# A trunk layer in three-pass float32 matmuls: rows for the MLP and gate stages turned by VectorE's 32x32 blocks and sixteen on-chip transfers instead of by TensorE

## Chip, cores and metric

One core of a Trainium2 chip. The metric is the device time of one execution in microseconds (us), the median of several runs.

## What is computed

One layer of a trunk for 256 tokens of width D = 2048, all in float32. The mixer is an attention with a compressed, a selected and a window branch; the change leaves it alone. After it come an MLP of width 8192 with a squared ReLU, and a gate on a projection of a 256-wide side input:

```python
def rms_norm(x, g):
    y = x * lax.rsqrt(jnp.mean(x * x, axis=-1, keepdims=True) + EPS)
    return y * g

h = x + nsa_mixer(rms_norm(x, norm_mix_g), ...)
u = rms_norm(h, norm_mlp_g)
h = h + jnp.square(jax.nn.relu(u @ mlp_w1)) @ mlp_w2
gate = jax.nn.sigmoid(rms_norm(h, ple_norm_g) @ ple_w_gate)
out = h + gate * (p @ ple_w_proj)
```

## The kernel before

Every large product is tokens x weights with the tokens on the partitions of the result. TensorE (PE) wants the activations with the feature on the partitions, so rows that one product leaves, or that an addition to `h` leaves, must be turned (transposed) before the next one reads them.

**Units and chunks.** A weight matrix is taken in chunks of 512 columns. A chunk is 8 units; a unit is 256 rows x 512 columns, 512 KB. Each float32 operand is split in two parts, hi and lo, and a product is three matmuls: hi x hi, hi x lo, lo x hi. For each unit SP loads `w_raw` (8 slots; `load`, L284 to L288, waits until `w_lo` of the unit 8 before is done), ACT copies it to `w_hi` (4 slots; `split_hi`, L436 to L448, waits until PE has used the unit 4 before), DVE makes `w_lo` by a subtraction (`split_lo`, L717 to L729), and PE runs 2 k-tiles x 2 token halves x 3 = 12 matmuls (`unit`, `half_unit`, `tile_product`, L1112) and counts `unit_used`. ACT, DVE and SP are each written out as a walk over the units, `for k in split_hi(...)`, with the other work of that engine hung on a number k: "k == 4" means right behind the split of unit 4 of that chunk. Each engine runs its own list in order. A wait is therefore also a wait for all that stands behind it on the same engine.

**Chunks around the change.** `C_OUT` to `C_OUT + 3` are the attention's output projection (its last two chunks are `C_OUT + 2` and `C_OUT + 3`); `C_MLP` on are the MLP: four quarters of 8 chunks, in each quarter four chunks up (w1, written to the hidden rows) and four down (w2, added to `h`); `C_PLE` to `C_PLE + 3` are the gate product, each with one more unit ahead of it for the projection of `p` (`ple_unit`, L1154).

**Turning rows.** There are three places. Output rows added to `h` by DVE (`add_to_h`, L908) are turned for the MLP: four sets, `R_H1`. The hidden rows, written to `stage` by ACT (`evac`, L455) and squared by POOL (L409), are turned for the way down: four sets in each quarter, `R_MLP`. The rows of `h` after the last quarter are turned for the gate: four sets, `R_H2`. A set is 512 features of 256 tokens. PE turns it with 8 transposes of 128x128 against an identity into the PSUM banks `tr` (`transpose_set`, `transpose_bank`, L1165), mostly at k == 2 of the chunk that follows. ACT makes the hi part out of `tr` (`transposed_hi`, L463 and L468, at k == 4), DVE the lo part (`transposed_lo`, L737 and L742, at k == 4). With a norm's gain these are four instructions of 128x256 on each engine, without it two of 128x512. Sets 0 and 1 of `R_H1` are turned in chunk `C_OUT + 2`, set 2 in `C_OUT + 3`, set 3 in `C_MLP`; set j of `R_MLP` in the chunk behind up chunk j. PE waits for them by pairs of units (`split_by`): unit k of the consuming chunk needs set k // 2. So in `C_MLP`, in the first down chunk of each quarter and in `C_PLE`, set 3 is turned in the very chunk whose unit 6 reads it.

## Time and profile before

| | |
|---|---|
| median of 3 runs | 1243.33 us (1242.25 to 1243.96) |
| the profiled execution | 1243.53 us |
| its span, first to last instruction | 1241.8 us |
| PE busy in the span | 1231.8 us, 99% |
| DVE, ACT, POOL busy | 700.6 us, 571.5 us, 57.5 us |
| weight loads of a unit, issue to landing | 3.7 us |

The span is what the trace shows; the 1.7 us between it and the execution's time lie ahead of the first instruction and behind the last. In the rows below L stands for a line of the kernel, `x` and a number for how many instructions a row joins, and SPq for DMAs that SP issues.

### The profile page before, as it was taken

The page shows a single profiled execution, that of the slowest core. Times are in us where ns is not written, and L with a number is a line of the kernel's source. Part 1 is how long each engine was busy: PE and PEld are TensorE (multiplying, and loading weights), DVE is VectorE, ACT ScalarE, POOL GpSimd, SP SyncE. Part 2 cuts the span into 40 slices and gives each one's busy share as a digit, 9 for nine tenths or more (in the row PEclk, how much of TensorE's full clock was granted, in tenths as well). Part 3 has the DMA queues.
Part 4 walks back from the last instruction along what each step waited for, and adds up shares of the span by engine and source line. Part 5 has one row for each costly group of instructions (what it writes and reads, how often), then busy time and mean ns, then how long its engine had stood idle before and what let it go on. Part 6 is the DMA issues. An engine that isn't in the chain of part 4 may idle for free.

```text
span 1241.8 us, 16004 instructions
## 1 busy us (share of the span) xinstructions
PE 1231.8 (99%) x5831; PEld 1019.3 (82%) x5831; DVE 700.6 (56%) x966; ACT 571.5 (46%) x784; POOL 57.5 (5%) x57
## 2 busy tenths in 40 slices
PE   8999999999999999999999999999999999999998
PEld 7888788888888888888878888888888888888886
DVE  5676546887765645554445454454545445555654
ACT  7554433554445544433444443444433445445543
POOL 0001000000000001000010000000000001000000
PEclk9999999999999999999999999999999999999999
DMA  9767664333335665556655556665556665555551
GB/s 335 205 191 210 200 173 138 116 104 103 102 119 187 183 193 182 188 194 196 193 168 194 189 191 194 184 188 190 189 191 193 186 191 184 182 192 174 203 195 63
DMA packets 123741, 222.07 MB, mean 179 GB/s; under 512 B 8996, under 2 KB 18584, under 8 KB 123672
## 3 DMA queue, kind: packets, MB, share of 16 engines
q1 hardware_dynamic: 123128, 220.55, 56.3%
q8 instruction: 52, 0.85, 0.3%
q10 hardware_dynamic: 544, 0.52, 0.2%
q14 instruction: 17, 0.14, 0.0%
HBM read 218.95 MB, written 2.10 MB: 178 GB/s over the span
## 4 chain that ended last, share of the span: by engine, by line
PE 97%; DVE 1%; POOL 1%; DMA 0%; issue 0%; ACT 0%; ACTq 0%
PE acc L1112 87%; PE tr L1165 2%; PE sc L1232 1%; POOL rs L395 1%; PE sc L1245 1%; PE sc L1231 1%; DVE w_lo L728 0%; PE tr L1154 0%; PE sc L1154 0%; PE acc L1139 0%; PE tr L1283 0%; PE tr L1279 0%; PE tr L1280 0%; DMA h<-in_x_dram 0%; PE tr L1259 0%; PE tr L1264 0%
## 5 line engine op out<-in xcount | busy, mean ns | idle before, releaser
L728 DVE TENSOR_TENSOR w_lo<-w_raw,w_hi 128x1024 fp32r<-128x1024 f32 x412 | 507.9, 1239 | 440.4 <-ACT w_hi L447 437.4
L447 ACT ACTIVATE w_hi<-w_raw 128x1024 fp32r<-128x1024 f32 x412 | 434.2, 1059 | 436.7 <-PE acc L1112 431.5
L1112 PE MATMUL acc<-w_hi,a_hi 128*128 128x512 f32 x958 | 383.1, 400 | 2.2 <-issue 1.5
L1112 PE MATMUL acc<-w_hi,a_lo 128*128 128x512 f32 x958 | 373.4, 390 | 0.0
L1112 PE MATMUL acc<-w_lo,a_hi 128*128 128x512 f32 x958 | 373.0, 389 | 0.0
L1112 PE MATMUL acc<-w_hi,b_hi 128*128 128x512 f32 x640 | 254.4, 398 | 0.0
L1112 PE MATMUL acc<-w_hi,b_lo 128*128 128x512 f32 x640 | 249.3, 390 | 0.0
L1112 PE MATMUL acc<-w_lo,b_hi 128*128 128x512 f32 x640 | 249.0, 389 | 0.0
L1112 PEld LDWEIGHTS acc<-w_hi,a_hi 128*128 128x128 f32 x958 | 180.1, 188 | 42.7 <-issue 3.8
L1112 PEld LDWEIGHTS acc<-w_lo,a_hi 128*128 128x128 f32 x958 | 180.1, 188 | 37.8 <-issue 2.4
L1112 PEld LDWEIGHTS acc<-w_hi,a_lo 128*128 128x128 f32 x958 | 179.8, 188 | 38.1
L1112 PEld LDWEIGHTS acc<-w_lo,b_hi 128*128 128x128 f32 x640 | 120.3, 188 | 25.6 <-issue 1.4
L1112 PEld LDWEIGHTS acc<-w_hi,b_hi 128*128 128x128 f32 x640 | 120.2, 188 | 25.4 <-issue 1.2
L1112 PEld LDWEIGHTS acc<-w_hi,b_lo 128*128 128x128 f32 x640 | 120.1, 188 | 25.3
L409 POOL TENSOR_TENSOR stage<-stage 128x512 f32<-128x512 f32 x32 | 32.6, 1040 | 588.8 <-ACT stage L455 588.8
L455 ACT ACTIVATE stage<-acc,rstd 128x512 f32<-128x512 f32 x48 | 30.3, 684 | 31.0 <-PE acc L1112 29.3
L737 DVE TENSOR_TENSOR b_lo<-tr,b_hi 128x512 fp32r<-128x512 f32 x32 | 20.6, 686 | 23.3 <-ACT b_hi L463 23.3
L463 ACT ACTIVATE b_hi<-tr 128x512 fp32r<-128x512 f32 x32 | 17.4, 596 | 33.3 <-PE tr L1165 33.3
L509 ACT ACTIVATE s<-s,nmx 128x128 f32<-128x128 f32 (+1 forms) x64 | 28.2, 445 | 4.6 <-DVE nmx L850 4.6
L908 DVE TENSOR_TENSOR h<-acc,h 128x512 f32<-128x512 f32 x40 | 25.7, 685 | 7.2 <-PE acc L1112 7.2
L395 POOL TENSOR_TENSOR rs<-ms,minus_half 128x8 f32<-128x8 f32 (+1 forms) x7 | 17.4, 2489 | 260.4 <-DVE ms L762 260.4
L517 ACT ACTIVATE p_t<-tr 128x512 f32<-128x512 f32 x16 | 9.6, 597 | 42.5 <-PE tr L1260 42.5
(171 smaller groups left out, 611.8 us busy)
## 6 DMA issues: line engine op xcount, KB each, us to landing
w_raw<-in_mlp_w_dram SPq DMA_DIRECT2D x256, 512.0 KB, 3.7
w_raw<-in_nsa_w_in_dram SPq DMA_DIRECT2D x79, 512.0 KB, 3.8
w_raw<-in_nsa_w_out_dram SPq DMA_DIRECT2D x32, 512.0 KB, 3.7
w_raw<-in_ple_w_gate_dram SPq DMA_DIRECT2D x32, 512.0 KB, 4.0
w_raw<-in_nsa_cmp_w_dram SPq DMA_DIRECT2D x8, 512.0 KB, 4.8
w_raw<-in_ple_w_proj_dram SPq DMA_DIRECT2D x4, 512.0 KB, 4.1
out_dram<-h SPq DMA_DIRECT2D x7, 256.0 KB, 4.3
h<-in_x_dram SPq DMA_DIRECT2D x3, 512.0 KB, 8.5
```

What stands on the lines that cost most here:

```text
L395: nc.gpsimd.tensor_tensor(o, ms[0:rows, 0:cols], minus_half[0:rows, 0:cols], ALU.pow).then_inc(rs_ready, 1)
L409: nc.gpsimd.tensor_tensor(stage[:, t], stage[:, t], stage[:, t], ALU.mult)\
L447: nc.scalar.activation(w_hi[:, u % SPLIT, 0:width], w_raw[:, u % RAW, 0:width], ACT.Copy).then_inc(hi_done, 1)
L455: nc.scalar.activation(dst(t), acc[c % 2][t][:], func, scale=scale[:, t:t + 1])\
L463: last = nc.scalar.activation(dst_hi[:, kt0 + 2 * b:kt0 + 2 * b + 2].rearrange("p k s -> p (k s)"), tr[b][:], ACT.Copy)
L509: last = nc.scalar.activation(s, s, ACT.Exp, bias=nmx[:, par, 2 * t + br:2 * t + br + 1], scale=SCALE, accum_out=sm[:, par, 2 * t + br:2 * ...
L728: nc.vector.tensor_tensor(w_lo[:, u % SPLIT, 0:width], w_raw[:, u % RAW, 0:width], f32(w_hi[:, u % SPLIT, 0:width]), ALU.subtract).then_in ...
L737: last = nc.vector.tensor_tensor(flat(lo, kt0 + 2 * b, 2), tr[b][:], f32(flat(hi, kt0 + 2 * b, 2)), ALU.subtract)
L908: nc.vector.tensor_tensor(cols, acc[c % 2][t][:], cols, ALU.add).then_inc(acc_read[c % 2][t], 1)
L1112: last = nc.tensor.matmul(acc[c % 2][t][:], xs[:, kt, toks], ws[:, u % SPLIT, m * NW:(m + 1) * NW], start=(kt == 0 and n == 0), stop=(kt = ...
L1165: last = nc.tensor.transpose(tr[b][:, m * SEQ + t * P:m * SEQ + (t + 1) * P], src(t, 2 * b + m), ident[:])
L1231: nc.tensor.matmul(sc[0][:, 0:SEQ], q_t[:, j, 0:P], keys[:, 0:SEQ], start=True, stop=True)
```

## The change

The 24 sets `R_H1`, `R_MLP` and `R_H2` are no longer turned on PE. For each set:

1. DVE turns the 32x32 blocks inside each 128x128 tile (`turn_blocks`: two `transpose` instructions of 128x512, one for each token half) and writes them, arranged by target quarter, to `blocks` (the tile `junk`). It first waits until the moves of the set before have landed.
2. SP issues sixteen DMAs, one for each pair of a source and a target quarter of 32 partitions (`turn_across`), from `blocks` to `turned` (the tile `q_t`). Each moves 32 partitions x 2 x 128 float32, 32 KB. They stand in the same queue as the weight loads.
3. ACT makes hi out of `turned`, DVE lo (`turned_gain`: four instructions of 128x256 each; `turned_hidden`: one of 128x1024 each), now at k == 6 or 7 instead of 4.
4. PE waits for a count of finished sets (`turned_by`) where it waited for `tr_done`.

`turned` and `blocks` exist once. SP's nested loops over chunks are written out by quarter so that the moves can stand inside them.

```diff
+            def turn_across(n, i=0):
+                sp.wait_ge(blocks_turned, TT * (n + 1 + 4 * i))
+                if n < T_HID and n > 0:
+                    sp.wait_ge(turned_split, n)
+                for a in range(P // QUAD):
+                    for b in range(P // QUAD):
+                        sp.dma_start(turned[b * QUAD:(b + 1) * QUAD].rearrange("i (t a f) -> i t a f", t=TT, f=P)[:, :, a],
+                                     blocks[a * QUAD:(a + 1) * QUAD].rearrange("i (b t f) -> i b t f", t=TT, f=P)[:, b])\
+                          .then_inc(turn_in, 16)
+            def turn_steps(k, turn, i=0):
+                for n, at in turn:
+                    if k == at:
+                        turn_across(n, i)
...
+                    if n == 3:
+                        turn_steps(k, ((T_H1, 2), (T_H1 + 1, 7)))
...
+            up_chunk(0, 0, ((T_H1 + 2, 4),))
+            up_chunk(1, 0, ((T_H1 + 3, 2),))
+            with sp.Fori(0, QUARTERS - 1) as q:
+                for j in (2, 3):
+                    up_chunk(j, q, up_turn(j - 2))
+                for j in range(4, 8):
+                    down_chunk(j, q, up_turn(j - 2) if j < 6 else ())
+                for j in (8, 9):
+                    up_chunk(j, q)
+            last_q = QUARTERS - 1
+            for j in (2, 3):
+                up_chunk(j, last_q, up_turn(j - 2))
+            for j in range(4, 8):
+                down_chunk(j, last_q, up_turn(j - 2) if j < 6 else down_turn(T_H2 + j - 6 - 4 * last_q))
...
+                    if n < 2:
+                        turn_steps(k, ((T_H2 + 2 + n, 1),))
...
+            def turned_gain(n, dst_hi, kt0, gain):
+                act.wait_ge(turn_in, 16 * MOVES * (n + 1))
+                for m in range(NW // P):
+                    last = nc.scalar.activation(tokens(dst_hi[:, kt0 + m]), turned_tile(m), ACT.Copy,
+                                                scale=const_t[:, gain + kt0 + m:gain + kt0 + m + 1])
+                last.then_inc(turned_hi, 1)
+            def turned_hidden(j, i):
+                act.wait_ge(turn_in, 16 * MOVES * (T_HID + j + 1 + 4 * i))
+                nc.scalar.activation(b_hi[:, 4 * j:4 * j + 4].rearrange("p m (g j) -> p m g j", j=QUAD),
+                                     turned.rearrange("p (g m j) -> p m g j", m=NW // P, j=QUAD),
+                                     ACT.Copy).then_inc(turned_hi, 1)
...
             for k in split_hi(FIRST[C_OUT + 2], UPC):
                 if k in (1, 2):
                     h_chunk_stats(C_OUT + k - 1, 1, k - 1)
-                if k in (4, 6):
-                    n = k // 2 - 2
-                    transposed_hi(R_H1 + n, a_hi, 4 * n, GAIN_MLP)
+                if k == 6:
+                    turned_gain(T_H1, a_hi, 0, GAIN_MLP)
             for k in split_hi(FIRST[C_OUT + 3], UPC):
                 if k == 2:
+                    turned_gain(T_H1 + 1, a_hi, 4, GAIN_MLP)
                     h_chunk_stats(C_OUT + 2, 1, 2)
-                if k == 4:
-                    transposed_hi(R_H1 + 2, a_hi, 8, GAIN_MLP)
+                if k == 6:
+                    turned_gain(T_H1 + 2, a_hi, 8, GAIN_MLP)
             for k in split_hi(FIRST[C_MLP], UPC):
                 if k == 2:
                     h_chunk_stats(C_OUT + 3, 1, 3)
-                if k == 4:
-                    transposed_hi(R_H1 + 3, a_hi, 12, GAIN_MLP)
+                if k == 6:
+                    turned_gain(T_H1 + 3, a_hi, 12, GAIN_MLP)
...
-                            transposed_hi(R_MLP + j - 1, b_hi, 4 * (j - 1), None, i)
+                        if k == 7:
+                            turned_hidden(j - 1, i)
...
+                    if k == 6:
+                        turned_gain(T_H2 + n, a_hi, 4 * n, GAIN_PLE)
...
+            def turn_blocks(n, src, i=0):
+                if not (isinstance(i, int) and n == 0):
+                    dve.wait_ge(turn_in, 16 * MOVES * (n + 4 * i))
+                for t in range(TT):
+                    nc.vector.transpose(
+                        blocks.rearrange("p (b t m j) -> p t m b j", b=P // QUAD, t=TT, j=QUAD)[:, t],
+                        src(t).rearrange("p (m b i) -> p m b i", b=P // QUAD, i=QUAD)).then_inc(blocks_turned, 1)
+            def turned_gain(n, hi, lo, kt0, gain):
+                dve.wait_ge(turned_hi, n + 1)
+                for m in range(NW // P):
+                    kt = kt0 + m
+                    last = nc.vector.scalar_tensor_tensor(
+                        out=tokens(lo[:, kt]), in0=turned_tile(m), scalar=const_t[:, gain + kt:gain + kt + 1],
+                        in1=tokens(f32(hi[:, kt])), op0=ALU.mult, op1=ALU.subtract)
+                last.then_inc(turned_split, 1)
+            def turned_hidden(j, i):
+                dve.wait_ge(turned_hi, T_HID + j + 1 + 4 * i)
+                hi, lo = (x[:, 4 * j:4 * j + 4].rearrange("p m (g j) -> p m g j", j=QUAD) for x in (b_hi, b_lo))
+                nc.vector.tensor_tensor(lo, turned.rearrange("p (g m j) -> p m g j", m=NW // P, j=QUAD), f32(hi),
+                                        ALU.subtract).then_inc(turned_split, 1)
...
             for k in split_lo(FIRST[C_OUT + 2], UPC):
                 if k in (1, 2):
...
-                if k in (4, 6):
-                    n = k // 2 - 2
-                    transposed_lo(R_H1 + n, a_hi, a_lo, 4 * n, GAIN_MLP)
+                if k == 2:
+                    dve.wait_ge(acc_read[(C_OUT + 1) % 2][TT - 1], (C_OUT + 1) // 2 + 1)
+                    turn_blocks(T_H1, h_rows(0))
+                if k == 5:
+                    turn_blocks(T_H1 + 1, h_rows(1))
+                if k == 7:
+                    turned_gain(T_H1, a_hi, a_lo, 0, GAIN_MLP)
             for k in split_lo(FIRST[C_OUT + 3], UPC):
                 if k == 2:
                     add_to_h(C_OUT + 2, 2)
-                if k == 4:
-                    transposed_lo(R_H1 + 2, a_hi, a_lo, 8, GAIN_MLP)
+                    dve.wait_ge(acc_read[C_OUT % 2][TT - 1], (C_OUT + 2) // 2 + 1)
+                    turn_blocks(T_H1 + 2, h_rows(2))
+                if k == 3:
+                    turned_gain(T_H1 + 1, a_hi, a_lo, 4, GAIN_MLP)
+                if k == 7:
+                    turned_gain(T_H1 + 2, a_hi, a_lo, 8, GAIN_MLP)
             for k in split_lo(FIRST[C_MLP], UPC):
                 if k == 2:
                     add_to_h(C_OUT + 3, 3)
+                    dve.wait_ge(acc_read[(C_OUT + 3) % 2][TT - 1], (C_OUT + 3) // 2 + 1)
+                    turn_blocks(T_H1 + 3, h_rows(3))
                 if k == 3:
                     mean_square(8, 1)
-                if k == 4:
-                    transposed_lo(R_H1 + 3, a_hi, a_lo, 12, GAIN_MLP)
+                if k == 7:
+                    turned_gain(T_H1 + 3, a_hi, a_lo, 12, GAIN_MLP)
...
                         if k == 4:
-                            transposed_lo(R_MLP + j - 1, b_hi, b_lo, 4 * (j - 1), None, i)
+                            dve.wait_ge(squared, TT * j + 4 * TT * i)
+                            turn_blocks(T_HID + j - 1, lambda t: stage[:, t], i)
+                        if k == 7:
+                            turned_hidden(j - 1, i)
...
+                        dve.wait_ge(acc_read[c % 2][TT - 1], c // 2 + 1)
+                        turn_blocks(T_H2 + n, h_rows(n))
...
-                    if k == 4:
-                        transposed_lo(R_H2 + n, a_hi, a_lo, 4 * n, GAIN_PLE)
+                    if k == 7:
+                        turned_gain(T_H2 + n, a_hi, a_lo, 4 * n, GAIN_PLE)
...
+            def turned_by(n, k, i=0):
+                pe.wait_ge(turned_split, n + k // 2 + 1 + 4 * i)
...
             for n in (2, 3):
                 c = C_OUT + n
                 for k in range(UPC):
-                    if k == 2:
-                        staged(c - 2 if n == 2 else c - 1)
-                        transpose_set(R_H1 + (0 if n == 2 else 2), from_h(0 if n == 2 else 2))
-                    if k == 4 and n == 2:
-                        staged(c - 1)
-                        transpose_set(R_H1 + 1, from_h(1))
                     unit(c, FIRST[c] + k, k, b_hi, b_lo)
             for k in range(UPC):
-                if k == 2:
-                    staged(C_OUT + 3)
-                    transpose_set(R_H1 + 3, from_h(3))
-                split_by(R_H1, k)
+                turned_by(T_H1, k)
                 unit(C_MLP, FIRST[C_MLP] + k, k, a_hi, a_lo)
...
-                        if k == 2:
-                            pe.wait_ge(squared, TT * j + 4 * TT * i)
-                            transpose_set(R_MLP + j - 1, from_stage, i)
                         if j == 4:
-                            split_by(R_MLP, k, i)
+                            turned_by(T_HID, k, i)
...
-                    if k == 2:
-                        staged(c - 1)
-                        transpose_set(R_H2 + n, from_h(n))
...
-                    if n == 0 and k == 2:
-                        staged(c - 1)
-                        transpose_set(R_H2 + 3, from_h(3))
                     if n == 0:
-                        split_by(R_H2, k)
+                        turned_by(T_H2, k)
```

**SP's queue, from chunk `C_OUT + 2` to the MLP.** `w_raw` are weight loads, `q_t<-junk` the moves of a set. Before, the whole output projection is one run of loads:

```order
L288 DMA w_raw<-in_nsa_w_out_dram 128x2x512 [waits lo_done] x32
```

and now:

```order
L308 DMA w_raw<-in_nsa_w_out_dram 128x2x512 [waits lo_done] x27
L317 DMA q_t<-junk 32x2x128 [waits blocks_turned]
L317 DMA q_t<-junk 32x2x128 x15
L308 DMA w_raw<-in_nsa_w_out_dram 128x2x512 [waits lo_done] x5
L317 DMA q_t<-junk 32x2x128 [waits turned_split,blocks_turned]
L317 DMA q_t<-junk 32x2x128 x15
L308 DMA w_raw<-in_mlp_w_dram 128x2x512 [waits lo_done] x5
L317 DMA q_t<-junk 32x2x128 [waits turned_split,blocks_turned]
L317 DMA q_t<-junk 32x2x128 x15
L308 DMA w_raw<-in_mlp_w_dram 128x2x512 [waits lo_done] x6
L317 DMA q_t<-junk 32x2x128 [waits turned_split,blocks_turned]
L317 DMA q_t<-junk 32x2x128 x15
L308 DMA w_raw<-in_mlp_w_dram 128x2x512 [waits lo_done] x5
```

Loads run 8 units ahead of the split, so the moves of set 0 stand between the loads of units 2 and 3 of `C_OUT + 3`, behind the splits of `C_OUT + 2`. Sets 1, 2 and 3 follow after 5, 5 and 6 more loads, and each of these waits for DVE's lo part of the set before as well.

**ACT in chunk `C_OUT + 3`.** `w_hi` is the split of a unit, `a_hi` the hi part of a set, `junk_act,ss<-h` the sums of squares. Before, from unit 0 of the chunk (`raw_full1`) to unit 6 (`raw_full7`):

```order
L447 ACTIVATE w_hi<-w_raw 128x1024 [waits unit_used,raw_full1]
L447 ACTIVATE w_hi<-w_raw 128x1024 [waits unit_used,raw_full2]
L447 ACTIVATE w_hi<-w_raw 128x1024 [waits unit_used,raw_full3]
L475 ACTIVATE junk_act,ss<-h 128x512 [waits acc_read11,acc_read10]
L475 ACTIVATE junk_act,ss<-h 128x512 [waits act_step]
L447 ACTIVATE w_hi<-w_raw 128x1024 [waits unit_used,raw_full4,act_step]
L447 ACTIVATE w_hi<-w_raw 128x1024 [waits unit_used,raw_full5]
L468 ACTIVATE a_hi<-tr,const_t 128x256 [waits tr_full0]
L468 ACTIVATE a_hi<-tr,const_t 128x256
L468 ACTIVATE a_hi<-tr,const_t 128x256 [waits tr_full1]
L468 ACTIVATE a_hi<-tr,const_t 128x256
L447 ACTIVATE w_hi<-w_raw 128x1024 [waits unit_used,raw_full6]
L447 ACTIVATE w_hi<-w_raw 128x1024 [waits unit_used,raw_full7]
```

and now, from the same unit on:

```order
L515 ACTIVATE w_hi<-w_raw 128x1024 [waits unit_used,raw_full1]
L515 ACTIVATE w_hi<-w_raw 128x1024 [waits unit_used,raw_full2]
L515 ACTIVATE w_hi<-w_raw 128x1024 [waits unit_used,raw_full3]
L544 ACTIVATE a_hi<-q_t,const_t 128x256 [waits turn_in]
L544 ACTIVATE a_hi<-q_t,const_t 128x256 x3
L558 ACTIVATE junk_act,ss<-h 128x512 [waits acc_read11,acc_read10]
L558 ACTIVATE junk_act,ss<-h 128x512 [waits act_step]
L515 ACTIVATE w_hi<-w_raw 128x1024 [waits unit_used,raw_full4,act_step]
L515 ACTIVATE w_hi<-w_raw 128x1024 [waits unit_used,raw_full5]
L515 ACTIVATE w_hi<-w_raw 128x1024 [waits unit_used,raw_full6]
L515 ACTIVATE w_hi<-w_raw 128x1024 [waits unit_used,raw_full7]
L544 ACTIVATE a_hi<-q_t,const_t 128x256 [waits turn_in]
```

The hi part of set 1 has moved into this chunk, between the splits of units 2 and 3 and ahead of the sums of squares; the one of set 2 stands behind the split of unit 6, where it stood behind that of unit 4.

**DVE in the up chunks of the last quarter.** `w_lo` is the split of a unit, `b_lo` the lo part of a set. Before:

```order
L728 TENSOR_TENSOR w_lo<-w_raw,w_hi 128x1024 [waits hi_done] x5
L737 TENSOR_TENSOR b_lo<-tr,b_hi 128x512 [waits tr_hi0]
L737 TENSOR_TENSOR b_lo<-tr,b_hi 128x512 [waits tr_hi1]
L728 TENSOR_TENSOR w_lo<-w_raw,w_hi 128x1024 [waits hi_done] x8
L737 TENSOR_TENSOR b_lo<-tr,b_hi 128x512 [waits tr_hi0]
```

and now:

```order
L811 TENSOR_TENSOR w_lo<-w_raw,w_hi 128x1024 [waits hi_done] x5
L836 STREAM_TRANSPOSE junk<-stage 128x4x4x32 [waits turn_in,squared]
L836 STREAM_TRANSPOSE junk<-stage 128x4x4x32
L811 TENSOR_TENSOR w_lo<-w_raw,w_hi 128x1024 [waits hi_done] x3
L854 TENSOR_TENSOR b_lo<-q_t,b_hi 128x1024 [waits turned_hi]
L811 TENSOR_TENSOR w_lo<-w_raw,w_hi 128x1024 [waits hi_done] x5
```

The blocks are turned where the lo part stood, behind unit 4, and the lo part has moved behind unit 7.

## Rows read from the trace of the kernel before

**Rows 1.** The page, parts 1 and 2: span, busy time, granted clock in 40 slices.

```profile
span 1241.8 us, 16004 instructions
...
PE 1231.8 (99%) x5831; PEld 1019.3 (82%) x5831; DVE 700.6 (56%) x966; ACT 571.5 (46%) x784; POOL 57.5 (5%) x57
...
PEclk9999999999999999999999999999999999999999
```

**Rows 2.** The page, part 4: the chain that ended last.

```profile
PE 97%; DVE 1%; POOL 1%; DMA 0%; issue 0%; ACT 0%; ACTq 0%
```

**Rows 3.** The waits of PE: for whom, us in total, times, longest.

```profile
PE sc L1313 <- POOL ident L378: 2.0, 1, 2.0
...
PE acc L1112 <- DVE w_lo L728: 0.8, 3, 0.3
```

**Rows 4.** The chain in order of time, from 370: start, us, what.

```profile
381.03 0.87 PE tr L1165 x8
...
428.12 21.79 PE acc L1112 x96
```

**Rows 5.** Instructions on tile tr: ns min/median/max, first and last start.

```profile
L1165 PE MATMUL tr<-ident,stage x192: 270/272/327, 44.6 to 1053.6; 128*128 128x128 f32 x192
...
L1165 PE MATMUL tr<-ident,h x96: 270/272/474, 3.8 to 1147.0; 128*128 128x128 f32 x96
```

**Rows 6.** SP, line L288: ns min/median/max of an issue, starts.

```profile
L288 SPq DMA_DIRECT2D w_raw<-in_mlp_w_dram x256: 372/373/392, 393.6 to 1107.3; - x128
...
L288 SPq DMA_DIRECT2D w_raw<-in_nsa_cmp_w_dram x8: 367/368/368, 55.0 to 91.9; - x8
```

**Rows 7.** SP in order of time at the kernel's start: start, us, what.

```profile
8.93 0.42 SPq L301 DMA_DIRECT2D const_rows<-in_ple_norm_g_dram  x1
9.40 0.33 SPq L301 DMA_DIRECT2D const_rows<-in_nsa_q_g_dram  x1
...
10.05 0.62 SPq L301 DMA_DIRECT2D const_rows<-in_nsa_cmp_pos_dram  x1
```

**Rows 8.** DMA issues by tensor: KB each, median us from issue to landing.

```profile
w_raw<-in_mlp_w_dram SPq DMA_DIRECT2D x256, 512.0 KB, 3.7
...
w_raw<-in_nsa_cmp_w_dram SPq DMA_DIRECT2D x8, 512.0 KB, 4.8
...
out_dram<-h SPq DMA_DIRECT2D x2, 128.0 KB, 1.8
...
const_rows<-in_norm_mix_g_dram SPq DMA_DIRECT2D x1, 8.0 KB, 2.2
```

**Rows 9.** DVE by line and shape: count, busy us, mean ns, idle before.

```profile
L728 DVE TENSOR_TENSOR w_lo<-w_raw,w_hi 128x1024 fp32r<-128x1024 f32 x411 | 506.9, 1240 | 439.4 <-ACT w_hi L447 436.4
L908 DVE TENSOR_TENSOR h<-acc,h 128x512 f32<-128x512 f32 x40 | 25.7, 685 | 7.2 <-PE acc L1112 7.2
...
L895 DVE COPY p_t<-tr 128x256 f32<-128x256 f32 x16 | 6.8, 424 | 7.8 <-PE tr L1266 7.8
```

**Rows 10.** DVE in order of time from 370: start, us, line, what.

```profile
378.03 1.28 DVE L908 TENSOR_TENSOR h<-acc,h 128x512 f32<-128x512 f32 x2
...
384.29 1.65 DVE L742 SCALAR_TENSOR_TENSOR a_lo<-tr,const_t,a_hi 128x256 fp32r<-128x256 f32 x4
```

**Rows 11.** ACT in order of time from 370.

```profile
374.28 0.63 ACT L475 ACTIVATE junk_act<-h 128x512 f32<-128x512 f32 x1 [2.98 <-DVE h L908]
...
375.57 0.19 ACT L475 ACTIVATION_READ_ACCUMULATOR junk_act<-h 128x1 f32 x1
...
382.83 1.55 ACT L468 ACTIVATE a_hi<-tr,const_t 128x256 fp32r<-128x256 f32 x4
```

**Rows 12.** ACT by line and shape.

```profile
L447 ACT ACTIVATE w_hi<-w_raw 128x1024 fp32r<-128x1024 f32 x411 | 433.3, 1059 | 435.3 <-PE acc L1112 430.1 <-DMA w_raw<-in_nsa_w_in_dram 1.7 <-PE tr L1154 1.3
```

**Rows 13.** DVE in order of time from 444.

```profile
446.74 2.80 DVE L728 TENSOR_TENSOR w_lo<-w_raw,w_hi 128x1024 fp32r<-128x1024 f32 x2 [2.65 <-ACT w_hi L447]
```

**Rows 14.** POOL in order of time from 444.

```profile
445.27 2.04 POOL L409 TENSOR_TENSOR stage<-stage 128x512 f32<-128x512 f32 x2 [16.27 <-ACT stage L455]
```

More of the change, by code:

```diff
@@ L119 @@
 R_H1 = p_set(H - 1) + 1
-R_MLP = R_H1 + 4
-R_H2 = R_MLP + 4 * QUARTERS
 def hi_sets(r):
-    return r + 1 if r < R_X + 4 else 5 if r == R_P else r - R_H1 + 6
+    return r + 1 if r < R_X + 4 else 5
+T_H1 = 0
+T_HID = 4
+T_H2 = T_HID + 4 * QUARTERS
+QUAD = 32
+MOVES = (P // QUAD) ** 2
 GAIN_MIX, GAIN_MLP, GAIN_PLE, GAIN_Q, GAIN_K, POS = 0, KT, 2 * KT, 3 * KT, 3 * KT + 1, 3 * KT + 4
@@ L260, in trunk_layer @@
         out_ready = sem("out_ready")
+        blocks_turned = sem("blocks_turned")
+        turn_in = sem("turn_in")
+        turned_hi = sem("turned_hi")
+        turned_split = sem("turned_split")
+        blocks = junk[:]
+        turned = q_t[:].rearrange("p j s -> p (j s)")
         block = ctx.enter_context(nc.Block())
@@ L270, in out_bank, with turned_tile, tokens @@
             return sc[0] if hh % HPG == 2 else tr[0]
+        def turned_tile(m):
+            return turned.rearrange("p (g m j) -> p m g j", m=NW // P, j=QUAD)[:, m]
+        def tokens(x):
+            return x.rearrange("p (g j) -> p g j", j=QUAD)
         def flat(x, kt0, n):
@@ L746, in transposed_lo, with h_rows @@
                     last.then_inc(tr_done[b], 1)
+            def turn_blocks(n, src, i=0):
[18 more added lines that the diff above has]
+                                        ALU.subtract).then_inc(turned_split, 1)
+            def h_rows(n):
+                return lambda t: h[:, t, n * NW:(n + 1) * NW]
             def mean_square(n, norm):
```

32 lines of the change are left out of this document (15 added, 17 removed).

## The prediction

> **What bounds the kernel now.** I read the page first. PE is busy 1231.8 us of a span of 1241.8 [rows 1], and the chain that ended last is PE for 97% [rows 2]. The waits of PE agree: the longest is 2.0 us at the start, and for a split weight it waited 0.8 us in all [rows 3]. So every microsecond taken off PE's list comes off the end, as long as its inputs are there. The chain in order of time [rows 4] shows what is taken off: a piece of 0.87 us of eight transposes, then 96 matmuls (8 units) in 21.79 us, that is 2.72 us a unit. ACT, DVE and SP have slack, but in their own order. The question is only whether a set that takes a longer way is there when PE, or a split queued behind it, wants it.
>
> **What is removed.** The transposes on `tr` that turn rows are 192 + 96 [rows 5]. Of these 288 the change takes 24 sets x 8 = 192; a set is one piece of 0.87 us in the chain [rows 4]. 24 x 0.87 = **-20.9 us**. ACT's and DVE's hi and lo parts keep about their length; DVE gains the block transposes, SP 24 x 16 = 384 issues. DVE is busy 56%, ACT 46% [rows 1], so the work itself is hidden, and what counts is when it stands.
>
> **The length of a turn.** No row of before shows this path, so I bound it.
>
> *VectorE's blocks*: two instructions of 128x512. The nearest rows are a tensor_tensor of 128x512 at 0.685 us and a copy of 128x256 at 0.424 [rows 9]. I take 0.69 each, 1.38 for a set; the ends are 0.42 (the shorter row) and 1.24 (the row of 128x1024). The Trainium skill's page "VectorE: DVE Perf Modes", section "The three transpose paths", gives 311 ns for a 128x128 bf16 tile turned by 32x32 blocks; four of those are 1.24 us, and by it the sum would come out near zero. No run here shows a block transpose yet.
>
> *Sixteen issues on SP*: an issue takes 0.367 to 0.373 us, for long rows (w1) as for the 512-byte pieces of the compressor's weights [rows 6]. In the start's burst an issue follows its predecessor after 0.05 us (8.93 + 0.42, then 9.40), and one of 32 KB in 64 rows took 0.62 [rows 7]. I take 0.41 a move (0.37 and a gap), as its form is that of the loads; ends 0.37 and 0.62. Fifteen periods: 6.15 us.
>
> *The last one's landing*: an 8 KB load landed 2.2 us after its issue began, a 128 KB store 1.8 [rows 8]. I take 1.96. The data is not the limit by these rows: 512 KB in 512-byte pieces (`cmp_w`) land within 4.8 us against 3.7 for long ones [rows 8], and the sixteen take 6.6 to issue.
>
> So from turned blocks to landed rows it is 6.15 + 1.96 = **8.1 us**, where PE and `tr` needed 0.9.
>
> **Where that is too long.** Times on the trace's clock, PE running without its transposes. ACT's hi part of a set takes about 1.57 us, DVE's lo part 1.66 [rows 10, 11], a split 1.06 and 1.24 [rows 9, 12], the sums of squares 1.48 (374.28 to 375.76) [rows 11].
>
> *`C_OUT + 2`* starts on PE at 381.03 - 2 x 2.72 = 375.6. `h` is ready at 379.3 [rows 10], blocks 380.7, landed 388.8, hi 390.4, ACT's split of unit 7 at 391.4, DVE's 392.7, lo part of set 0 at 394.3. PE wants unit 7 at 394.6, so it just holds. Blocks of set 1 wait on DVE for set 0 to land: DVE's unit 6 is ready at 391.5, wanted at 391.9.
>
> *Set 1* may be moved only now: it lands at 402.4. On ACT it stands ahead of the sums and of the split of unit 3 of `C_OUT + 3`: hi 404.0, sums 405.5, split 406.5, DVE 407.8, with some ten hand-overs of 0.05 us 408.2. PE wants that unit at 375.6 + 11 x 2.72 = 405.5: **2.7 us stall**, and 0.2 at the next unit, since DVE's lo part of set 1 stands between.
>
> *Set 2*'s moves stand behind the load that waits for DVE's unit 4 (411.1): landed 419.7, hi 421.3, split of unit 7 422.4, DVE 423.7. PE wants it at 408.4 + 4 x 2.72 = 419.3: **4.4 us**, and again 0.2.
>
> *Set 3*, in `C_MLP` (from 426.6): DVE does lo of set 2, three splits, the addition and the blocks until 431.8; landed 439.9, hi 441.5, split of unit 7 442.6, DVE 443.8, lo 445.6. PE wants the set at its unit 6, 426.6 + 16.3 = 442.9: **2.7 us**.
>
> *Hidden rows.* In a chunk that starts at 0 (444.46 in the trace, two units ahead of the set at 449.91, where the run of 96 in rows 4 ends), POOL is through at 2.9 [rows 14] and DVE's unit 4 at 5.1 [rows 13], so POOL isn't what ends last. Blocks 6.5, landed 14.6, hi as one 128x1024 on ACT (1.06) 15.7, lo (1.24) 17.0. Sets 0 to 2 have a chunk or more of room. Set 3 is wanted at unit 6, 16.3: **0.7 us, four times = 2.8**. The split of the next chunk's unit 0 is pushed from 14.7 to 16.8 on ACT and 18.3 on DVE, wanted at 21.8: covered, with 3.5 us left.
>
> *Gate rows.* Sets 0 to 2 land in time. Set 3 in `C_PLE`: blocks 2.7, but the moves stand behind a load that waits for DVE's split of unit 3, 5.6; landed 13.8, hi 15.4, split 16.5, 17.7, lo 19.4, wanted at 2.8 + 16.3 = 19.1: **0.5 with hand-overs**.
>
> *SP's other work.* A turn holds the weight loads behind it for about 8 us; a load is wanted some 20 us after its slot is free and takes 3.7 [rows 8]. Covered twice over.
>
> **Sum.** -20.9 + (2.7 + 0.2 + 4.4 + 0.2 + 2.7) + 2.8 + 0.5 = -7.4 us on the profiled execution's 1243.5: **1236.1 us** (the median of before is 0.2 lower). Nine places decide (unit 6 of `C_OUT + 2`, units 3 and 7 of `C_OUT + 3`, set 3 in `C_MLP`, in the four quarters and in `C_PLE`): each further 1 us in a turn costs about 8 to 9 us, and each one less gives as much back until the quarters and the gate have no stall.
>
> **The rivals.**
>
> *A. The turn is shorter, and only the first chunks stall.* With 0.37 a move, the turn is 0.6 us shorter: -7.4 - 5.4 = -12.8. Shorter blocks too (0.42) take 0.54 off those places where the blocks come late: down to about -16, since the moves of set 2 stay behind the split of unit 4. 1227 to 1231 us, less if an issue is shorter than any seen. For it: the store's issue and landing are the shortest of their kind. Against it: every issue of this form shows 0.367 at least.
>
> *B. VectorE's blocks take 1.24 us.* A set's blocks come 1.1 us later in the quarters, at the first chunk and at set 3: about seven places, +7.7. The time is 1243.8, no change. For it: a turned read fills and drains blocks, and the write is scattered in runs of 32. Against it: other strided forms here cost no more than dense ones. The Trainium skill's figure, cited above, is this case.
>
> *C. The moves are slower than they look, and the kernel is slower.* The mechanism is the burst: sixteen DMAs from one quarter to one quarter behind each other back up SP's queue or land late. It decides from 0.8 us more in a turn, that is 0.47 us a move or a landing after 2.8. At 0.62 a move [rows 7] a turn is 3.2 us longer: 9 x 3.2 = +28, with the sum +21, 1265 us. For it: that row, and issues of 0.58 us and more in the start's burst. Against it: those stood behind megabytes of loads, here at most one load of 512 KB is under way. In its hardest form each move lands before the next starts: 16 x 1.8 us [rows 8] is 29 us a set, longer than a chunk, some 24 chunks grow by 8 us, near 1430 us. Loads that come every 2.72 us and take 3.7 to land [rows 4, 8] overlap, so this form has 0.02 within C. The Trainium skill's page "DMA: Bandwidth & Descriptors", section "Rules for kernel authors", says that two transfers to disjoint partition halves serialize and that below 64 KB one pays mostly overhead, which speaks for C; the trace has no pair of transfers to disjoint quarters.
>
> *D. PE's clock.* It is granted in full in all slices [rows 1], but PE never idled over 2.0 us [rows 3], and now it would for 4.4. A fall to 1.2 GHz would make a unit of 2.72 us cost up to 2.7 more; one or two units after each of three stalls are 3 to 8 us. This is a price inside the main case and C, and pulls both up.
>
> That the change doesn't take the transposes off PE can be left out: its list has none of the 192 left.
>
> **The numbers.** Main case (-14 to -3 us) 0.50; A beyond it 0.13; B, within 0.2% (2.5 us, about what a measurement of this kernel can tell from none) 0.12; C with D 0.25. The forecast is 1236.1. For 8 in 10 the range runs from 1226 (most of A is inside) to 1255 (half of C is inside). Faster 0.63, same 0.12, slower 0.25.
>
> **What would show it.** Right: PE's list without L1165 after 375; chunks of the way down at 21.8 us with nothing between; DMAs `q_t<-junk` about 0.41 us apart and landed 8 us after the blocks; ACT and DVE waiting for DMA at the hi parts; PE waits of 2 to 5 us at three places between 400 and 445, under 1 us once in each quarter. Wrong: block transposes much over 0.7 us, moves further apart than 0.47, waits of PE in chunks without a set due, a clock under 1.0 behind a stall.

## The result: 1296.75 us, slower by 4.3%, and the profile after

The changed kernel takes 1296.75 us (median of four runs, 1294.78 to 1297.45) against 1243.47 us for the kernel before beside it: ratio 1.0427, 95% interval 1.0414 to 1.0440. The forecast was 1236.1 us, with a range from 1226 to 1255. The profiled execution's span is 1295.1 us.

The page of the kernel after: span, busy time, granted clock in 40 slices, the chain that ended last, the moves' landing.

```profile
span 1295.1 us, 15768 instructions
...
PE 1235.0 (95%) x5639; PEld 1012.2 (78%) x5639; DVE 730.3 (56%) x998; ACT 566.0 (44%) x768; POOL 81.2 (6%) x57
...
PEclk9999999999999989989999999999899999899899
...
PE 65%; SPq 13%; DVE 6%; issue 4%; ACT 4%; DMA 3%; POOL 3%; ACTq 0%; DVEq 0%; POOLq 0%
...
q_t<-junk SPq DMA_DIRECT2D x384, 32.0 KB, 1.9
```

PE has 192 instructions fewer than in [rows 1], as announced. But the chain, PE for 97% in [rows 2], is now PE for 65% and SP's queue for 13%: SP issues DMAs, so somebody waits for issues. PE's busy time has not fallen although its list is shorter, because the granted clock has dips: the same 5639 instructions keep PE busy for 1209.9 us in `e2_four` below, where the clock is full, and for 1235.0 here, 25 us longer.

The waits of PE after (us in total, times, longest), and those of ACT:

```profile
PE acc L1240 <- DVE w_lo L811: 21.7, 16, 6.7
PE acc L1240 <- DVE b_lo L854: 19.8, 4, 5.5
PE acc L1240 <- DVE a_lo L845: 9.8, 2, 5.2
```

```profile
ACT b_hi L551 <- DMA q_t<-junk: 105.4, 16, 7.6
ACT a_hi L544 <- DMA q_t<-junk: 65.5, 8, 13.1
```

In [rows 3] PE waited 0.8 us for splits; now it is 51 us. ACT stands at every one of the 24 turns, up to 13.1 us long, and the weight splits queued behind it stand too, which fits the 16 waits for `w_lo`.

One line of the moves (issue time in ns, min/median/max), and VectorE's blocks:

```profile
L317 SPq DMA_DIRECT2D q_t<-junk x384: 586/597/1790, 382.1 to 1201.4; - x192
```

```profile
L836 DVE STREAM_TRANSPOSE junk<-stage x32: 660/684/705, 474.3 to 1092.0; 128x512 f32<-128x512 f32 x32
```

The blocks take 0.68 us, as forecast (0.69). The landing is 1.9 us, as forecast (1.96). The issue is 0.60 us, not 0.37, and a move follows the last after 0.64 us, as the chain in order of time shows (start, us, what). It also shows the first three turns behind each other:

```profile
390.54 0.60 SPq L317
391.18 0.60 SPq L317
391.82 1.85 DMA q_t<-junk
394.11 1.29 ACT a_hi L544 x3
395.40 0.96 ACT w_hi L515
396.38 1.22 DVE w_lo L811
397.60 1.59 DVE a_lo L845 x4
399.91 0.60 SPq L317
...
409.46 1.83 DMA q_t<-junk
411.73 1.29 ACT a_hi L544 x3
...
416.73 1.58 DVE a_lo L845 x4
...
429.52 1.89 DMA q_t<-junk
```

The last moves of sets 0, 1 and 2 have landed at 393.7, 411.3 and 431.4; the forecast had 388.8, 402.4 and 419.7. Of each delay 1.3 us stood before any turn (PE began `C_OUT + 2` at 376.9 in this execution, the forecast has 375.6). The rest is 3.6, 7.6 and 10.4: it grows from set to set, since a turn starts only when the lo part of the one before is done. For set 2 one more split and one weight load, at 418.31 and 419.48 in the chain, stand between.

### The profile page after: what moved, and what is told of

Its sections match the earlier page's. It is cut to its first block, busy times and chain, and to the rows that moved or that the text cites. A ratio compares the mean times of both kernels' runs of the same rounds, so it can differ in the third digit from the quotient of the medians.

```text
span 1295.1 us, 15768 instructions
## 1 busy us (share of the span) xinstructions
PE 1235.0 (95%) x5639; PEld 1012.2 (78%) x5639; DVE 730.3 (56%) x998; ACT 566.0 (44%) x768; POOL 81.2 (6%) x57
## 4 chain that ended last, share of the span: by engine, by line
PE 65%; SPq 13%; DVE 6%; issue 4%; ACT 4%; DMA 3%; POOL 3%; ACTq 0%; DVEq 0%; POOLq 0%
PE acc L1240 57%; SPq L317 13%; DMA q_t<-junk 3%; ACT w_hi L515 2%; POOL stage L477 2%; DVE w_lo L811 2%; DVE junk L836 2%; PE sc L1364 1%; PE tr L1293 1%; DVE a_lo L845 1%; ACT a_hi L544 1%; DVE b_lo L854 1%; ACT b_hi L551 1%; POOL rs L463 1%; PE sc L1377 1%
## 5 line engine op out<-in xcount | busy, mean ns | idle before, releaser
L515 ACT ACTIVATE w_hi<-w_raw 128x1024 fp32r<-128x1024 f32 x412 | 428.2, 1055 | 382.0 <-PE acc L1240 377.4
L1240 PE MATMUL acc<-w_hi,b_hi 128*128 128x512 f32 x640 | 261.1, 408 | 38.0 <-DVE b_lo L854 19.8
L1240 PE MATMUL acc<-w_hi,b_lo 128*128 128x512 f32 x640 | 254.5, 398 | 0.0
L1240 PE MATMUL acc<-w_lo,b_hi 128*128 128x512 f32 x640 | 254.4, 397 | 0.0
L1240 PEld LDWEIGHTS acc<-w_hi,b_hi 128*128 128x128 f32 x640 | 123.8, 193 | 70.3 <-DVE w_lo L811 21.2
L477 POOL TENSOR_TENSOR stage<-stage 128x512 f32<-128x512 f32 x32 | 56.3, 1778 | 586.7 <-ACT stage L523 586.7
L854 DVE TENSOR_TENSOR b_lo<-q_t,b_hi 128x1024 fp32r<-128x1024 f32 x16 | 19.6, 1226 | 102.7 <-ACT b_hi L551 102.7
L551 ACT ACTIVATE b_hi<-q_t 128x1024 fp32r<-128x1024 f32 x16 | 17.0, 1060 | 105.4 <-DMA q_t<-junk 105.4
L544 ACT ACTIVATE a_hi<-q_t,const_t 128x256 fp32r<-128x256 f32 x32 | 13.6, 497 | 65.5 <-DMA q_t<-junk 65.5
L523 ACT ACTIVATE stage<-acc,rstd 128x512 f32<-128x512 f32 x48 | 30.2, 679 | 11.5 <-PE acc L1240 9.7
```

Of the source, the lines that this page charges most:

```text
L477: nc.gpsimd.tensor_tensor(stage[:, t], stage[:, t], stage[:, t], ALU.mult)\
L515: nc.scalar.activation(w_hi[:, u % SPLIT, 0:width], w_raw[:, u % RAW, 0:width], ACT.Copy).then_inc(hi_done, 1)
L523: nc.scalar.activation(dst(t), acc[c % 2][t][:], func, scale=scale[:, t:t + 1])\
L544: last = nc.scalar.activation(tokens(dst_hi[:, kt0 + m]), turned_tile(m), ACT.Copy, scale=const_t[:, gain + kt0 + m:gain + kt0 + m + 1])
L551: nc.scalar.activation(b_hi[:, 4 * j:4 * j + 4].rearrange("p m (g j) -> p m g j", j=QUAD), turned.rearrange("p (g m j) -> p m g j", m=NW / ...
L854: nc.vector.tensor_tensor(lo, turned.rearrange("p (g m j) -> p m g j", m=NW // P, j=QUAD), f32(hi), ALU.subtract).then_inc(turned_split, 1)
```

## Where the time is, place by place

PE's products into `acc` are the same in all kernels, 96 to a chunk, so the time from the first product of a chunk to the first of the next can be laid side by side. With nothing in the way a hidden or output chunk takes 21.8 us and a gate chunk, with its ninth unit, 24.6. Kernel `e2_four` below has that everywhere around the change; the table gives what each kernel takes more than it (us, from the starts of the matmuls in the traces). "Read after" is how long after the start of the second of VectorE's two blocks instructions ScalarE began to read the set, for the last hidden set of the kernel (after: 1092.0 to 1104.4).

```
                     read    C_OUT+2,    4th set   other   down chunks,  C_PLE   sum   median us
                     after   +3, C_MLP   x 4       hidden  last quarter
forecast              8.8      10.2       2.8       0        0            0.5    13.5   1236.1
e2_four               6.3       0         0         0        0            0       0     1220.64
e3_hbm                9.4      13.8       6.2       0        0            1.5    21.5   1244.44
e5_bounce            10.8      11.6      13.1       0        0            2.5    27.2   1248.68
e8_half              11.2      20.2      16.9       0.8      0            5.9    43.8   1267.81
e7_later             12.2      27.1      25.3       0        3.8          8.6    64.8   1286.62
e4_fill              12.3      23.9      26.0      13.3      2.8          7.5    73.5   1291.55
after                12.4      26.9      29.5       6.2      4.3          7.9    74.8   1296.75
e10_hybrid            -         2.7       3.6       0        0            0.9     7.2   1228.27
```

The columns of the first chunks, the 4th set and `C_PLE` hold the forecast's nine places; the other two it had at nothing. The sums, added to `e2_four`, account for the medians to within 3.5 us.

## The experiments

**The form of a move.** Rows go across as 256 consecutive floats instead of two pieces of 128; the set's rows then stand in another order, so the output is not the reference's.

```
- turned[...].rearrange("i (t a f) -> i t a f", t=TT, f=P)[:, :, a], blocks[...].rearrange("i (b t f) -> i b t f", ...)[:, b]
+ turned[...].rearrange("i (a g) -> i a g", g=TT * P)[:, a],         blocks[...].rearrange("i (b g) -> i b g", ...)[:, b]
```

> The changed kernel with each move written as one run of 256 elements a partition (32x256) instead of 2 x 128; the rows arrive in another order, so the turned rows are wrong, and the work is the same. In the changed kernel a move's issue takes 0.60 us. If the three-dimensional form is what costs, the issue falls to about 0.33 to 0.37, a turn to 8 us, and the time to about 1240. If it is that the source lies in SBUF or that only 32 partitions are moved, the issue stays at 0.60 and the time at about 1297.

Measured: 1289.55 us in a single run, 7 us below the changed kernel; why is open. The issue is 0.591 us in the median against 0.597, so the shape of the pieces is not what makes it long.

**Four moves.** `sp.dma_start` once for each `a` over all 128 partitions, so no row changes its quarter (the rows of a set are wrong) and 16 issues become 4.

> The changed kernel with four moves a set, each of all 128 partitions and 2 x 128 elements, without the crossing of quarters (the turned rows are wrong, the bytes are the same). If the source in SBUF is what makes an issue 0.60 us, it stays 0.60 here; if it is the 32 partitions, it falls to 0.37. Either way a turn is 3 x 0.64 + 1.9 = 3.8 us or less, no set is late, the clock stays full, and by the sum of the prediction without its stalls the time is 1243.5 - 20.9 = 1222.6 us. A rival, that the work on ACT, DVE and POOL itself has become too much, gives over 1230.

Measured: 1220.64 us (1220.02 to 1221.62), ratio 0.9816 [0.9800, 0.9833]. Its page, the waits of PE and its moves:

```profile
PEclk9999999999999999999999999999999999999999
```

```profile
PE acc L1239 <- DVE w_lo L810: 0.6, 2, 0.3
```

```profile
L316 SPq DMA_DIRECT2D q_t<-junk x96: 605/622/712, 380.8 to 1123.3; - x96
```

With a short turn the whole gain appears, 23.2 us against 1243.81 for before beside it: the 20.9 us of transposes and some 2 us more. The issue over 128 partitions takes the same 0.62 us, so what costs is the number of issues.

**Moves from HBM.** The same sixteen moves with the same destinations, but read from the input `x` in HBM (the rows are wrong).

> The changed kernel with the sixteen moves of 32x2x128 read from x in HBM instead of from the turned blocks (the turned rows are wrong). If an SBUF source costs the issue 0.60 us, it falls to 0.37 here and a turn lasts about 8.1 us, the length that the prediction reckoned with: then the time tests the rest of its sum, 1236 us, more if the clock falls behind a stall of 4.4 us. If the 32 partitions cost, the issue stays 0.60 and the time at about 1297.

Measured: 1244.44 us (1242.7 to 1248.58), ratio 1.0008 [0.9998, 1.0018].

```profile
L317 SPq DMA_DIRECT2D q_t<-in_x_dram x384: 312/427/1407, 381.8 to 1149.8; - x192
```

Same count, bytes and destination, and the same landing (1.9 us in the median), but 0.43 us an issue where HBM is the source and 0.60 where SBUF is. That one difference is 52.3 us of time.

**Keeping PE awake.** In front of the eight longest waits PE does 30 transposes of the identity into a free bank.

```
+ def fill(n):
+     for _ in range(n):
+         nc.tensor.transpose(tr[0][:, 0:P], ident[:], ident[:])
```

> The changed kernel with 30 transposes of the identity on TensorE (about 3.3 us of work that nobody reads) ahead of each of the eight longest waits: units 3 and 7 of C_OUT + 3, unit 6 of C_MLP, of the four first down chunks, and of C_PLE. They fill time in which TensorE waits anyway. If about 25 us of the changed kernel's loss is the halved clock behind the stalls, the granted clock stays 1.00 and the time falls to about 1272. If the clock falls for another reason, or the fill delays the real work, it stays at 1297 or rises by up to 8 x 3.3 = 26.

Measured: 1291.55 us (1290.34 to 1294.12), ratio 1.0380 [1.0363, 1.0398]. From 400 to 475 the granted clock and PE's products, first of the kernel after, then of this one:

```profile
400.00:475.00 75.00, 58.74 (x228) 46.95 (x227) 34.74 (x45) 27.48 (x42) 3.64 (x3) 0.89 0.53 163
```

```profile
400.00:475.00 75.00, 68.14 (x338) 57.06 (x337) 36.26 (x45) 29.21 (x43) 3.64 (x3) 0.98 0.55 171
```

The clock came back in part and the time hardly: the mean rose from 0.980 to 0.992, and the time fell by 5.2 us of the 53. PE was busy for 1251.0 us, and less the 240 transposes of the fill (0.109 us each by [rows 4], 26 us) for about 1225: some 10 of the 25 us by which the low clock had stretched its work. In the table, which goes by the profiled executions (1294.1 us here), the columns of the nine places lose 6.9 us less than in the kernel after, but the other hidden chunks, which have no fill, lose 7.1 us more. So 5.2 us is the balance of the fill, not the price of the clock, which this run does not settle.

**A turn through HBM.** Four stores of 128 KB into a scratch tensor, a wait, two loads of 256 KB.

```
+ for a in range(P // QUAD):
+     sp.dma_start(scratch.rearrange("(b i) (a g) -> i b a g", i=QUAD, g=TT * P)[:, :, a],
+                  blocks[a * QUAD:(a + 1) * QUAD].rearrange("i (b g) -> i b g", g=TT * P)).then_inc(stored, 16)
+ sp.wait_ge(stored, 64 * (n + 1 + 4 * i))
+ for t in range(TT):
+     sp.dma_start(turned...[:, t], scratch.rearrange("p (a t f) -> p t a f", t=TT, f=P)[:, t]).then_inc(turn_in, 16)
```

> The changed kernel with one edit: a turn crosses the partition quarters through a scratch tensor in HBM, in four stores of 128 KB (32 partitions x 4 x 256 floats), a wait until they have landed, and two loads of 256 KB; 6 issues instead of 16. The output is the reference's. Theory 1 (the length of a turn is what costs: 16 issues of 0.64 us one after the other on SyncE's queue, then 1.9 us to land): the turn is 4 x 0.6 + 2.0 + 2 x 0.4 + 2.5 = 7.7 us instead of 12.1 us, that is shorter than the 8.8 us of the kernel whose moves came from HBM (1244.4 us) and longer than the 5.5 us of the four-move kernel (1220.6 us): 1232 to 1240 us, POOL's squares at 1040 ns again. Rival (the round trip through HBM adds its own landing in front of loads that also wait behind weight loads of 512 KB in the same queue, 4.1 us each): the turn stays at 11 us or more and the time at 1275 us or more.

Measured: 1248.68 us (1246.04 to 1251.94), ratio 1.0045 [1.0030, 1.0060], 8.7 us above the top of what was expected. Its DMAs by tensor (KB, median us to landing), and their issues:

```profile
turn_scratch<-junk SPq DMA_DIRECT2D x96, 128.0 KB, 3.2
q_t<-turn_scratch SPq DMA_DIRECT2D x48, 256.0 KB, 3.4
```

```profile
L318 SPq DMA_DIRECT2D turn_scratch<-junk x96: 327/436/1078, 381.2 to 1148.1; - x96
```

Both landings are longer than I had put in (3.2 and 3.4, not 2.0 and 2.5), and from turned blocks to landed rows it takes 7.7 to 11.1 us in the 21 turns whose stores start at once, 9.3 in the median, and only three of them take 7.8 or less. It still recovers 48 of the 53 us and the rival (1275 or more) is out. The stores read SBUF and are issued in 0.44 us: an SBUF source alone does not make an issue long. But the loads, which come from HBM, are issued as slowly as the moves:

```profile
L323 SPq DMA_DIRECT2D q_t<-turn_scratch x48: 523/611/640, 384.8 to 1152.2; - x48
```

So a move with SBUF at both ends is slow to issue from SP in every run here, 0.59 to 0.62 us whatever its shape, but it is not the only slow form, and what makes an issue long stays open.

**Later splits.** The first three hidden sets of a quarter are split one chunk later.

```
- if k == 7: turned_hidden(j - 1, i)
+ if k == 2 and j > 1: turned_hidden(j - 2, i)
+ if k == 7 and j == 4: turned_hidden(j - 1, i)
```

> The changed kernel with one edit: in the hidden chunks ScalarE and VectorE split the first three turned sets of a quarter one chunk later (before unit 2 of the next chunk instead of behind unit 7 of the same), so neither engine waits for a turn of 12 us there; only the fourth set still has to be waited for. Theory (a second part of the loss is that the two engines stand in their queues for a turn's end: 12 of the 16 hidden sets, after which VectorE's lo parts of the weights run beside POOL's squares, which take 2.0 instead of 1.04 us and hold the next set's blocks back): squares back to 1040 ns for most, the 12 waits of ScalarE for the moves gone, each quarter 3 to 6 us shorter, in all 1275 to 1285 us. Rival (only the fourth set, whose turn nothing covers, costs): the four quarters stay within 1 us each, 1293 to 1297 us.

Measured: 1286.62 us (1285.74 to 1288.87), ratio 1.0352 [1.0335, 1.0370]: 10.1 us less, 1.6 short of what was expected, against nothing by the rival. POOL's squares by line and shape (count, busy, mean ns, idle before), first after, then here:

```profile
L477 POOL TENSOR_TENSOR stage<-stage 128x512 f32<-128x512 f32 x32 | 56.3, 1778 | 586.7 <-ACT stage L523 586.7
```

```profile
L477 POOL TENSOR_TENSOR stage<-stage 128x512 f32<-128x512 f32 x32 | 32.6, 1040 | 598.3 <-ACT stage L523 598.3
```

The collision can be seen in the kernel after by itself, in POOL and then in DVE in order of time:

```profile
491.83 3.88 POOL L477 TENSOR_TENSOR stage<-stage 128x512 f32<-128x512 f32 x2 [19.72 <-ACT stage L523]
```

```profile
493.31 3.48 DVE L811 TENSOR_TENSOR w_lo<-w_raw,w_hi 128x1024 fp32r<-128x1024 f32 x2 [0.48 <-ACT w_hi L515]
496.72 1.29 DVE L836 STREAM_TRANSPOSE junk<-stage 128x512 f32<-128x512 f32 x2
```

Two squares took 2.04 us and two splits 2.80 from one start to the last end in [rows 13, 14]; side by side they take 3.88 and 3.48. As I read it, a late VectorE runs its splits beside the squares, those delay the next blocks, and the lateness keeps itself up from chunk to chunk; the run took away the stands and the collision together and does not part them. The Trainium skill's page "SBUF — State Buffer", section "Who interferes with whom", says that a VectorE instruction with two inputs in SBUF contends with a GpSimd instruction that reads SBUF; these rows agree.

**Half the dose.** Of the sixteen moves 8 read HBM and 8 the blocks.

> The changed kernel, but 8 of a turn's 16 moves read from the input in HBM (issue 0.43 us) and 8 from the blocks in SBUF (0.62 us), so the rows of the turned sets are partly wrong: a dose between the kernel with all 16 from HBM (1244.4 us) and the changed one (1296.75 us). The turn is 8 x 0.43 + 8 x 0.62 + 1.9 = 10.3 us, against 8.8 and 11.9. If the time goes straight with the length of a turn: 1270 us. If a threshold lies between them (VectorE late, so that POOL's squares double and hold up the next blocks): either near 1250 or near 1290 us, with the squares at 1040 or at 2018 ns.

Measured: 1267.81 us (1264.61 to 1271.57), ratio 1.0206 [1.0188, 1.0224], two us from the 1270 expected; POOL's mean is 1217 ns, so its squares have begun to slow. No single threshold lies between the two ends, but the line is not straight either: the 1270 rests on reckoned turns. By the table's measured 9.4, 11.2 and 12.4 us a straight line gives 1275.8, and the time rises by 13 us for each 1 us of turn up to here and by 24 beyond.

**Both edits**, through HBM and split later.

> Both edits together: the turn by four stores to HBM and two loads, and the first three hidden sets of a quarter split one chunk later. The output is the reference's. Theory: what is left is the uncovered turn of 7.7 us in nine places; 1230 to 1238 us, 0 to 3 us below the kernel with the stores and loads alone, since with so short a turn VectorE is no longer late. Rival (the turn through HBM is no shorter): as the kernel with the later splits alone, 1265 us or more.

Measured: 1248.74 us (1246.28 to 1253.38), ratio 1.0043 [1.0027, 1.0058]: nothing on top of the stores and loads alone. The squares were at 1050 ns there already, so there was nothing for the later splits to mend; my 1230 to 1238 rested on the turn of 7.7 us, which most turns exceed.

**A hybrid.** Only the 16 sets with room are turned the new way (the first of the MLP norm, three hidden sets of a quarter, three of the gate), and split a chunk later; the other 8 stay on TensorE. In the hidden chunks, on PE:

```
+ if j == 4 and k == 2:
+     pe.wait_ge(squared, TT * j + 4 * TT * i)
+     transpose_set(R_MLP, from_stage, i)
+ if j == 4 and k < 6: turned_by(T_HID, k, i)
+ elif j == 4:         split_by(R_MLP - 3, k, i)
```

> A version meant to beat both: only the 16 sets whose turn is covered by at least six units of 2.7 us are turned by VectorE and the sixteen moves (the first set of the MLP norm, the first three hidden sets of each quarter, the first three sets of the gate), and both engines split them one chunk later; the 8 sets that are needed at once (the other three of the MLP norm, the fourth hidden set of each quarter, the fourth of the gate) stay on TensorE as in the kernel before. The output is the reference's. Theory (the uncovered turns cost, and nothing else does): 16 x 0.87 = 13.9 us less than before, or 15.5 us at the 0.97 us a set that the four-move kernel gained: 1228 to 1230 us; the first two chunks behind the attention at 23 us again, no wait of TensorE for a turned set, squares at 1040 ns. Rival (the moves cost wherever they stand, since 16 issues of 0.64 us hold the weight loads behind them): 16/24 of the changed kernel's loss comes back, 1260 us or more.

Measured: 1228.27 us (1227.79 to 1228.75), ratio 0.9881 [0.9864, 0.9897]: faster than both, 14.6 us below before and 68 below the changed kernel. Its waits of PE for a split, and its moves:

```profile
PE acc L1247 <- DVE w_lo L819: 0.6, 2, 0.3
```

```profile
L321 SPq DMA_DIRECT2D q_t<-junk x256: 585/597/1721, 381.4 to 1113.0; - x128
```

Its 256 moves are as slow as ever and cost nothing that can be seen: its 7.2 us above `e2_four` are the 8 sets left on PE (8 x 0.87 = 7.0), and no engine waits for a move. That leaves the rival (moves cost wherever they stand) with nothing.

**The first four turns from GpSimd's queue**, so that no weight load stands behind them.

```
+ for n in range(4):
+     pool.wait_ge(blocks_turned, TT * (n + 1))
+     if n > 0:
+         pool.wait_ge(turned_split, n)
+     for a in range(P // QUAD):
+         for b in range(P // QUAD):
+             nc.gpsimd.dma_start(turned...[:, :, a], blocks...[:, b]).then_inc(turn_first, 16)
```

> The changed kernel, but the sixteen moves of the four sets of the MLP norm are issued by GpSimd instead of SyncE, so no weight load stands behind them; all else as in the changed kernel. The output is the reference's. Theory A (most of the 19 us lost in the two chunks behind the attention, 24.9 + 38.1 us instead of 21.8 + 21.8, come from weight loads that stand behind a turn in SyncE's queue: the waits for w_lo): the second chunk falls to 28 to 32 us and the time to 1285 to 1290 us. Theory B (the chain of four turns itself, each from VectorE's blocks over the moves to both splits, sets that time): it stays at 36 us or more and the time at 1292 to 1300 us, or above if GpSimd's own issues are slower than 0.64 us.

Measured: 1296.4 us (1295.12 to 1297.99), ratio 1.0425 [1.0408, 1.0442]; the first two chunks behind the attention take 29.9 + 33.7 us, together 63.6 against 63.0.

```profile
q_t<-junk POOLq DMA_DIRECT2D x64, 32.0 KB, 4.2
```

The second chunk's 33.7 us lies between the two theories (28 to 32, or 36 and more), but the first is 5 us longer, and the sum of the two chunks and the time are those of theory B. It is no clean cut, since an issue took less here (536 ns in the median) and a landing more (4.2 us instead of 1.9). The trace of the kernel after settles it better. There ScalarE's weight splits wait for a load three times in all, each time in the layer's first products, once in the line that does nearly all of them:

```profile
ACT w_hi L515 <- DMA w_raw<-in_nsa_w_in_dram: 1.1, 1, 1.1
```

No split waited for a load of the output projection, the MLP or the gate, so the loads behind the moves are not what held PE.

## Why the prediction was wrong

**What was removed**: right, and a little small. -20.9 us was announced, -23.2 shown with short turns (`e2_four`).

**VectorE's blocks**: right, 0.68 us against 0.69. Rival B (1.24 us) fell; that was my estimate, four times the 311 ns that the Trainium skill's page "VectorE: DVE Perf Modes", section "The three transpose paths", gives for a 128x128 bf16 tile.

**Sixteen issues on SP: the step that failed.** "I take 0.41 a move (0.37 and a gap), as its form is that of the loads". It was 0.64 from move to move, 9.6 us for fifteen periods instead of 6.15. I took my value from loads out of HBM, and the trace of before has no DMA with SBUF at both ends; the row at 0.62 [rows 7] was the one that came true, and it had a chance of 0.25 only. That row is a load from HBM at the kernel's start, so its number fits and no run shows that its reason is the same. The landing (1.96, measured 1.9) was right. By the prediction's own rule these 3.5 us more in a turn are worth about 30 of the 60.7 us by which the forecast was off; the other half is the rule, two paragraphs on.

**Where that is too long**: the places and the mechanism were right, as the kernel nearest to my turn shows. `e3_hbm` reads 9.4 us after the blocks where I had 8.8. Stalls of 13.5 us, and nine places times 0.6, would be 19; it has 21.5. The first chunks (10.2 forecast, 13.8 there) and C_PLE were a bit small.

**Nine places, 8 to 9 us for each 1 us of turn: the second step that failed.** From `e3_hbm` to the kernel after the turn grows by 3.0 us, worth 27 by that rule, and the time by 52, 17 for each 1 us. By the table 43 of it lie at the nine places and 10 in chunks that the forecast had at nothing. `e7_later` takes 10 us back: engines that stand at turns with room, and with them the squares beside the splits, which the prediction called "covered, with 3.5 us left". For the rest the clock is the candidate: the same list keeps PE busy 18.6 us longer than in `e3_hbm` (1235.0 against 1216.4). But the two parts overlap, the only run on the clock, `e4_fill`, brought a balance of 5 us, and so 10 to 15 us stay open. That ScalarE's stand at `a_hi` makes the waits for `w_lo` is read from the chain after, where `w_hi` and `w_lo` follow `a_hi` at once; no run has tried it by itself.

**SP's other work** ("covered twice over"): right, since in the kernel after no split waits for a load behind the moves.

**The rivals.** C with D (0.25, 1265 us) was the case that came, with its trigger as written, 0.62 a move; its price was 32 us too low. The Trainium skill's page "DMA: Bandwidth & Descriptors", section "Rules for kernel authors", spoke for C: below 64 KB one pays mostly overhead. Here 32 KB take 0.60 us to issue and 128 KB 0.62, which agrees. C's hardest form, each move landing before the next starts, did not come: most sets have landed 11.5 us after their blocks, not 29. D, PE's clock, was foreseen at 3 to 8 us. It stretched PE's own work by 25 us; what that costs in time, where PE also waits, is shown by no run. The granted clock by stretches of 25 us in the kernel after (us, busy PE, PEld, DVE, ACT, POOL, then PEclk) falls below full, in part to the lower level of 1.2 GHz, where the waits stand, and is whole where there are none:

```profile
375.00:400.00 25.00, 22.19 (x98) 18.04 (x98) 13.89 (x19) 13.23 (x21) 0.00 (x0) 1.00 0.50 159
400.00:425.00 25.00, 18.27 (x70) 14.54 (x69) 11.31 (x15) 7.26 (x13) 0.00 (x0) 0.86 0.51 157
...
575.00:600.00 25.00, 25.00 (x112) 20.71 (x111) 12.75 (x12) 9.55 (x9) 0.00 (x0) 1.00 0.58 196
```

## What to carry to other kernels

Price a chain of small transfers by count times the issue period of exactly that form, source and destination memory included; where no row has the form, let the longest row of its kind carry the sum, because sixteen repeats turn 0.2 us into 3.5. Move work off the bound engine only where its result has more room than the new path is long: here two thirds of the change, on the sets with room and with their splits a chunk later, gain 1.2%, and with the other third, and the splits where they were, it is a loss of 4.3%. In engines that work in order, put the consumer of a long transfer late enough that it never stands at it, since whatever is queued behind it pays too.
